# A layer with 32 sorted experts on one core: the choice of experts in two-operand steps, the rows sorted in two halves, five experts between

## What is computed

```python
def hierarchical_moe(h, w_router_group, b_router_group, w_router_expert, b_router_expert, w_gate, w_up, w_down):
    g_prob = softmax(t @ w_router_group + b_router_group)          # 4 groups
    g_p, g_idx = lax.top_k(g_prob, 1)
    e_logits = (t @ w_router_expert + b_router_expert).reshape(B * T, N_GROUPS, EXPERTS_PER_GROUP)
    e_in = jnp.einsum('ng,nge->ne', g_onehot, e_logits)            # the 8 experts of that group
    e_p, e_idx = lax.top_k(softmax(e_in), TOP_K_IN_GROUP)          # the best two, renormalised
    ...
    out = out + down(silu(t @ w_gate[e]) * (t @ w_up[e]) * combine[e])
```

## Time and profile before

| | |
|---|---|
| median of 3 runs | 869.36 us (866.34 to 869.45) |
| profiled execution | 869.71 us, span 867.8 us |
| PE, busy share of the span | 86% |
| DVE, ACT, POOL | 47%, 34%, 17% |
| DMA, mean over the span | 234 GB/s |
| DMA from about 650 us to 824 us | 416 to 420 GB/s |

### The profile page before, as it was taken

One profiled execution on the slowest core, in us unless ns is written; L12 is line 12 of the kernel. 1 busy time (PEld: TensorE's weight loads), 2 busy tenths in 40 slices (PEclk: granted clock), 3 DMA queues, 4 the chain that ended last, 5 costly groups with the idle time before them and its releaser, 6 DMA issues.

```text
span 867.8 us, 14573 instructions
## 1 busy us (share of the span) xinstructions
PE 750.1 (86%) x5476; PEld 598.7 (69%) x5476; DVE 403.9 (47%) x936; ACT 298.3 (34%) x550; POOL 143.9 (17%) x245
## 2 busy tenths in 40 slices
PE   2999999999888999998689999895789999778870
PEld 1899999997455698998577889894755555344430
DVE  3575324467444465665456567755652222111113
ACT  5433553556333264654322325444221111111110
POOL 5001000002233200232122100003012222211210
PEclk9999999999699999999999999997699999999995
DMA  5245243326587634535493637875399999999975
GB/s 185 98 147 182 97 147 122 122 97 204 150 243 209 198 135 146 191 117 190 151 299 127 220 107 261 352 297 216 147 374 416 419 418 418 419 420 419 419 284 188
DMA packets 38170, 202.84 MB, mean 234 GB/s; under 512 B 7490, under 2 KB 8018, under 8 KB 18898
## 3 DMA queue, kind: packets, MB, share of 16 engines
q1 hardware_dynamic: 24434, 160.29, 48.0%
q0 software_dynamic: 13664, 41.58, 15.0%
HBM read 184.24 MB, written 23.38 MB: 239 GB/s over the span
## 4 chain that ended last, share of the span: by engine, by line
PE 61%; DMA 16%; DVE 11%; ACT 5%; issue 5%; POOLq 0%; SPq 0%; POOL 0%; DVEq 0%; ACTq 0%
PE bank L1711 21%; PE bank L1715 10%; DMA fm<-in_w_moe 10%; PE bank L2059 7%; PE bank L1867 3%; PE bank L1701 3%; DMA em<-in_w_moe 3%; PE bank L2079 3%; DVE rm L1120 2%; ACT rm L797 2%; PE bank L1951 2%; PE bank L2040 2%; PE bank L1856 1%; DMA fm<-y_rows 1%; PE bank L1916 1%
## 5 line engine op out<-in xcount | busy, mean ns | idle before, releaser
L1711 PE MATMUL bank<-rm 128*128 128x320 f32 x1344 | 209.7, 315 | 1.6 <-ACT fm L825 1.6
L1711 PEld LDWEIGHTS bank<-rm 128*128 128x128 f32 x1344 | 201.3, 191 | 6.4 <-issue 3.7
L1120 DVE TENSOR_TENSOR rm<-fm,rm 128x2048 fp32r<-128x2048 f32 x48 | 110.0, 2292 | 71.1 <-ACT rm L797 70.6
L1715 PE MATMUL bank<-rm 128*128 128x256 f32 x960 | 122.2, 286 | 2.4 <-DVE fm L1491 2.4
L1715 PEld LDWEIGHTS bank<-rm 128*128 128x128 f32 x960 | 118.3, 193 | 3.3 <-issue 2.9
L2061 PE MATMUL bank<-fm,em 128*64 128x256 f32 x384 | 98.1, 401 | 0.0
L797 ACT ACTIVATE rm<-fm 128x2048 fp32r<-128x2048 f32 x48 | 91.9, 1915 | 17.1 <-PE bank L1711 11.2
L2059 PE MATMUL bank<-em 128*64 128x256 f32 x272 | 68.1, 395 | 12.9 <-DMA fm<-in_w_moe 7.9
L2059 PE MATMUL bank<-fm,em 128*64 128x256 f32 x240 | 60.3, 397 | 11.0 <-DMA fm<-in_w_moe 9.6
L2059 PEld LDWEIGHTS bank<-em 128*64 128x64 f32 x272 | 36.2, 140 | 40.2 <-issue 25.5
L1083 ACT ACTIVATE fm<-bank 64x256 f32<-64x256 f32 x32 | 12.0, 375 | 138.2 <-PE bank L2061 138.2
(11 more groups left out here) (391 smaller groups left out, 1010.5 us busy)
## 6 DMA issues: line engine op xcount, KB each, us to landing
fm<-in_w_moe SPq DMA_DIRECT2D x57, 1024.0 KB, 26.7
fm<-in_w_dense SPq DMA_DIRECT2D x48, 1024.0 KB, 4.9
em<-in_w_moe SPq DMA_DIRECT2D x39, 1024.0 KB, 25.7
fm<-in_state_C POOLq DMA_DIRECT2D x32, 257.0 KB, 4.4
out_C_sample<-fm POOLq DMA_DIRECT2D x32, 257.0 KB, 5.2
fm<-in_cache_v POOLq DMA_DIRECT2D x16, 512.0 KB, 4.6
fm<-in_cache_kT POOLq DMA_DIRECT2D x10, 512.0 KB, 5.8
em<-in_cache_kT POOLq DMA_DIRECT2D x6, 512.0 KB, 8.1
```

The costliest lines, as they stand in the source:

```text
L1120: s(TT(pair[c % 2][1], cube(raw[c % RAW1], KC), pair[c % 2][0], ALU.subtract), sem("split_done"))
L1711: ins = mm(bank[b][:, 0:NT], w[:, k, P * u:P * (u + 1)], a[:, k, :], start=first, stop=final)
L1715: ins = mm(bank[b][0:r, 0:CW], a[:, k, TILE0[u]:TILE0[u] + r], w[:, k, :], start=first, stop=final)
```

## The change

Four things are changed together.

1. **Choice of experts.** `gidx`, `eidx` and their casts are gone: the comparisons read the integer indices. The three `scalar_tensor_tensor` steps that push other groups down (one for each tile of tokens) become a product (`gneg` by a constant kept in `rb40`) and one sum over all three tiles.
2. **Low parts.** POOL makes the low part of `h2` for two tiles of tokens, DVE for the third (64 rows), after `gap`.
3. **Sort in two halves.** The one-hot rows are written by halves of 320 slots. PE sorts the first half (40 matmuls), expert 0 starts from it, and the second half is sorted in two pieces of 20 matmuls behind `down` of expert 1 and of expert 2, through banks 6 and 7. The offsets of experts 1 to 4 are limited so that their windows lie in the first half; from expert 5 on POOL waits for the whole of `xs`. DVE writes the second half's one-hot rows between its copies of the first half. The table of row numbers (L2098) goes behind `down` of expert 0, and the words for the end behind expert 1.
4. **Slots.** Loads 17 to 24 go into slots 0 to 7 again, each when its matrix is used up; 25 to 28 go to the memory of `h2s` and `onehot` when the second half is out (`xs_ready` at 2); later ones go round as before. Load 14 also waits for the first `onehot`. Small router tiles move from `fm` to that same memory.

```diff
@@ slots
+        NSLOT, NFREE, NAGAIN = len(slot), 17, 8
+        HALF, NBEFORE = SLOTS // 2, 5
+        h2s = [cube(rm[:, 0:3 * D], 3), cube(rm[:, 3 * D:5 * D], 2)]
+        def slot_of(n):
+            if n < NFREE:
+                return n
+            if n < NFREE + NAGAIN:
+                return n - NFREE
+            return n - NAGAIN if n < NSLOT + NAGAIN else slot_of(n - NSLOT)
@@ SP
-                    sp.wait_ge(sem("h2_split"), 3)
-                elif n == 17:
-                    sp.wait_ge(sem("sorted_full"), 2 * KC)
-                elif n >= NSLOT:
+                    sp.wait_ge(sem("h2_split"), 2)
+                    sp.wait_ge(sem("onehot"), 1)
+                elif n == NFREE + NAGAIN:
+                    sp.wait_ge(sem("xs_ready"), 2)
+                elif NFREE <= n < NFREE + NAGAIN:
+                    sp.wait_ge(sem("e_used"), n - NFREE + 1)
+                elif n >= NSLOT + NAGAIN:
@@ POOL
-            for t in range(3):
+            for t in range(2):
@@ ACT
+                if v in (2, 3):
+                    sorted_more((4 * (v - 2), 4 * (v - 2) + 2))
@@ DVE
-            s(CP(gidx, gi))
-            s(TT(ghot, iota[:, 0:NG].unsqueeze(1).broadcast_to([P, 3, NG]), gidx[:, :, 0:1].broadcast_to([P, 3, NG]),
+            s(TT(gneg, iota[:, 0:NG].unsqueeze(1).broadcast_to([P, 3, NG]), gi[:, :, 0:1].broadcast_to([P, 3, NG]),
                  ALU.not_equal))
+            s(TT(gneg, gneg, rb40[:, NG:NG + 1].unsqueeze(1).broadcast_to([P, 3, NG]), ALU.mult))
+            s(TT(esel.rearrange("p t (g e) -> p t g e", g=NG), gneg.unsqueeze(3).broadcast_to([P, 3, NG, EPG]),
+                 lg[:, :, 8:40].rearrange("p t (g e) -> p t g e", g=NG), ALU.add))
             for t in range(3):
-                s(STT(esel[:, t, :].rearrange("p (g e) -> p g e", g=NG),
-                      ghot[:, t, :].unsqueeze(2).broadcast_to([P, NG, EPG]), NEG,
-                      lg[:, t, 8:40].rearrange("p (g e) -> p g e", g=NG), ALU.mult, ALU.add))
                 s(v.max(etop[:, t, :], esel[:, t, :]))
                 s(v.max_index(ei[:, t, :], etop[:, t, :], esel[:, t, :]))
-            s(CP(eidx, ei))
...
+            dve.wait_ge(sem("h2_hi"), 3)
+            s(TT(h2s[0][NS:2 * NS, 2, :], h2[0:NS, 2, :], h2s[0][0:NS, 2, :], ALU.subtract))
...
+            for k in range(1, KC, 2):
+                dve.wait_ge(sem("sorted_full"), k + 1)
+                s(CP(xs[:, k, 0:HALF], bank[k % 4][:, 0:HALF]), sem("sorted_free_v"))
+                if k < 6:
+                    hot_slots(k // 2, 1)
+            dve.wait_ge(sem("sorted_free_a"), KC // 2)
+            s(v.tensor_reduce(most[:, 0:1], bank[4][:, 0:NE], AX_X, ALU.max), sem("xs_ready"))
...
+                if e in (2, 3):
+                    sorted_more((4 * (e - 2) + 1, 4 * (e - 2) + 3))
+                if e == 3:
+                    dve.wait_ge(sem("sorted_free_a"), KC)
+                    dve.wait_ge(sem("sorted_free_v"), KC)
+                    s(v.memset(xs[:, :, SLOTS:XC], 0.0), sem("xs_ready"))
@@ PE
             start(0)
-            pe.wait_ge(sem("onehot"), 3 + 6)
-            for k in range(2):
-                for t in range(3):
-                    i, r = 3 * k + t, ROWS[t]
-                    ins = mm(bank[6][0:CAP, 0:NE], at_rank[i][0:r, :], hot[k][0:r, t, :], start=(i == 0), stop=(i == 5))
-            ins.then_inc(sem("router_full"), 1)
...
                 down(4 + v % 2, htp[v % 2], weights(v, 2)).then_inc(sem("e_used"), 1)
+                if v == 0:
+                    row_table()
+                elif v in (1, 2):
+                    sort_more(range(4 * (v - 1), 4 * v))
```

More of the change, by code:

```diff
@@ L1065, in _, with sorted_more @@
             act.wait_ge(sem("x1_stored"), 16)
-            for n in range(0, 2 * KC, 2):
-                k, half = n // 2, n % 2
-                act.wait_ge(sem("sorted_full"), n + 1)
-                s(A_(xs[:, k, NT * half:NT * (half + 1)], bank[n % 4][:, 0:NT], ACT.Copy), sem("sorted_free_a"))
+            for k in range(0, KC, 2):
+                act.wait_ge(sem("sorted_full"), k + 1)
+                s(A_(xs[:, k, 0:HALF], bank[k % 4][:, 0:HALF], ACT.Copy), sem("sorted_free_a"))
+            def sorted_more(ks):
+                for k in ks:
+                    act.wait_ge(sem("sorted_full"), KC + k + 1)
+                    A_(xs[:, k, HALF:SLOTS], bank[6][:, 0:HALF], ACT.Copy).then_inc(sem("sorted_free_a"), 1)
             def take_y(v):
@@ L1566, in _, with hot_slots @@
             s(CP(place[NS:2 * NS, 2, :], place[0:NS, 2, :]))
+            def hot_slots(t, half):
+                w = slice(HALF * half, HALF * (half + 1))
+                s(TSC(onehot[:, t, w], iota[:, w], place[:, t, 0:1], None, ALU.is_equal))
+                s(STT(onehot[:, t, w], iota[:, w], place[:, t, 1:2], onehot[:, t, w], ALU.is_equal, ALU.add), sem("onehot"))
             for t in range(3):
-                s(TSC(onehot[:, t, :], iota, place[:, t, 0:1], None, ALU.is_equal))
-                s(STT(onehot[:, t, :], iota, place[:, t, 1:2], onehot[:, t, :], ALU.is_equal, ALU.add),
-                  sem("onehot"))
+                hot_slots(t, 0)
             dve.wait_ge(sem("router_full"), 5)
@@ L2034, in _, with sort, sort_more @@
                skip_group_check=True).then_inc(sem("router_full"), 1)
-            def sort(n, t):
-                k, half = n // 2, n % 2
+            def sort(b, k, half, t):
                 for i in range(2 if t < 2 else 1):
-                    ins = mm(bank[n % 4][:, 0:NT], h2s[i][:, t, P * k:P * (k + 1)],
-                             onehot[:, t, NT * half:NT * (half + 1)], start=(t == 0 and i == 0), stop=(t == 2))
+                    ins = mm(bank[b][:, 0:HALF], h2s[i][:, t, P * k:P * (k + 1)], onehot[:, t, HALF * half:HALF * (half + 1)],
+                             start=(t == 0 and i == 0), stop=(t == 2))
                 if t == 2:
                     ins.then_inc(sem("sorted_full"), 1)
+            pe.wait_ge(sem("h2_split"), 2)
             for t in range(3):
-                pe.wait_ge(sem("h2_split"), t + 1)
                 pe.wait_ge(sem("onehot"), t + 1)
-                for n in range(4):
-                    sort(n, t)
-            for n in range(4, 2 * KC):
-                pe.wait_ge(sem(("sorted_free_a", "sorted_free_v")[n % 2]), n // 2 - 1)
+                for k in range(4):
+                    sort(k, k, 0, t)
+            for k in range(4, KC):
+                pe.wait_ge(sem(("sorted_free_a", "sorted_free_v")[k % 2]), k // 2 - 1)
                 for t in range(3):
-                    sort(n, t)
+                    sort(k % 4, k, 0, t)
+            def sort_more(ks):
+                pe.wait_ge(sem("onehot"), 6)
+                for k in ks:
+                    if k >= 2:
+                        pe.wait_ge(sem(("sorted_free_a", "sorted_free_v")[k % 2]), KC // 2 + k // 2)
+                    for t in range(3):
+                        sort(6 + k % 2, k, 1, t)
             def gate_up(b, x, gate, up, between=None):
@@ L2091, in start, with row_table @@
                 last_u.then_inc(sem("e_used"), 1)
-            start(0)
-            pe.wait_ge(sem("onehot"), 3 + 6)
-            for k in range(2):
-                for t in range(3):
-                    i, r = 3 * k + t, ROWS[t]
-                    ins = mm(bank[6][0:CAP, 0:NE], at_rank[i][0:r, :], hot[k][0:r, t, :], start=(i == 0), stop=(i == 5))
-            ins.then_inc(sem("router_full"), 1)
+            def row_table():
+                pe.wait_ge(sem("onehot"), 6 + 6)
+                for k in range(2):
+                    for t in range(3):
+                        i, r = 3 * k + t, ROWS[t]
+                        ins = mm(bank[6][0:CAP, HALF:HALF + NE], at_rank[i][0:r, :], hot[k][0:r, t, :], start=(i == 0),
+                                 stop=(i == 5))
+                ins.then_inc(sem("router_full"), 1)
+            start(0)
             for v in range(NE):
```

87 lines of the change are left out of this document (42 added, 45 removed).

## The result

The changed kernel took 875.19 us in the median of five runs (871.57 to 876.79), the kernel before 869.36 (866.34 to 870.96). The ratio is 1.007, with a 95% interval of 1.0045 to 1.0095: 3.9 to 8.3 us slower. The forecast was 873.8 within 869.3 to 877.5.

What follows compares the result with a forecast made beforehand. The weight-load queue was taken to set the end, not PE: its last hole ends 4.4 us later, so the profiled 869.71 us becomes 874.1, and the median, 0.35 below, 873.8 us, within 869.3 to 877.5.

Steps and rivals of the forecast that it cites:

- (A): The forecast itself, the hole of the load queue at load 25: 2.5 to 6 us later, 55%.
- (C): Rival: PE's clock falls in a new pause, before expert 0 or 2: 875.5 for one, 877.2 for two, 17%.
- The choice: Choice of experts: new two-operand steps wait for POOL's low-part steps; chosen_r at 608.32 against 610.57, 2.25 us won.
- (B): Rival at the choice of experts: POOL spares the new steps, 3.16 us more won ahead of the sort, 870.6, 14%.
- The third low part: Low part moved to DVE, ahead of the sort: costs some 1.22 us, leaving 1.77 us of the 2.25 won.
- Expert 0: Start of the expert stage after the sort's first half: at 624.1 instead of 631.29, 7.2 us won.
- The queue: Weight loads: full flow at load 25 only at 656.2, 4.4 us later than before, after being idle twice.
- the table of rows ... expert 2 starts at 12.0 ... 30.45: Sum from expert 0's start to the second `xs_ready`: 30.45 us, with PE waiting 1.8 before expert 2.
- The instant to beat: When load 24 was in before the change, 71 loads being left: 651.8, with some 0.2 us for rows of `y_rows`.
- PE's own pace: PE in the expert stage: `down(3)` ends at 658.7 against 659.85, 1.1 us earlier, then starves later all the same.
- (D): Rival in the expert stage: PE, not the queue, sets the end, so the 1.1 us count, 868.3, 6%.
- (E): Rival: something faster that no row shows; over 0.5% needs load 25 flowing by 647.4, expert 0 at 615.3, 8%.

Runs made afterwards that it cites:

- three_operands: The changed kernel with the choice's product and sum as three scalar_tensor_tensor steps again, casts still gone: 875.29 us, ratio 1.0095.
- choice_only: The kernel before with the two-operand choice of experts alone, POOL keeping all three low parts, sort whole: 865.9 us, ratio 0.9965.
- sort_first: The kernel before with the new choice of experts and the third low part on DVE, sort whole: 865.77 us, ratio 0.9971.
- sort_first_pieces: The kernel before with the two-operand choice, third low part on DVE, POOL's low parts in eight pieces, sort whole: 866.09 us, ratio 0.9965.
- onehot_after: The changed kernel with the second half's one-hot rows written after the four copies of the first half, not between them: 874.32 us, ratio 1.0088.
- combined: The changed kernel with the second half one expert earlier, POOL's low parts in eight pieces and one-hot rows after the copies: 866.08 us, ratio 0.999.
- low_part_pieces: The changed kernel with POOL's two low-part steps of 128x1024 cut into eight of 128x256: 872.88 us, ratio 1.0076.
- early_filled: The changed kernel with second half one expert earlier, POOL's eight pieces, one-hot rows moved to DVE's waits, eight unread matmuls before expert 0: 864.85 us, 0.9947.

## Why the prediction was right, and where it was off

The direction, the range and the mechanism were right. The time alone doesn't tell (A) from (C), since 875.19 is inside the range of (A), 871.9 to 875.4, and 0.3 below what (C) gives for one fall; the traces do. The case that I called likeliest, (A) with the clock up, was not the regular one, and what I had as rival (C), at 17%, is.

**The choice.** Right in each step: 1.43 and 2.30 us for steps that need 0.2, the second spared in the gap, `chosen_r` within 0.13. `three_operands` shows that the form of the step doesn't matter. Rival (B) is out: in the rows shown, steps beside a step of POOL waited until it ended, and only those in the gap between two of its steps were spared. The Trainium skill's "SBUF — State Buffer", "Who interferes with whom", has the blocked step wait until the first is done; the traces agree, with the ends 0.05 us apart in `three_operands`. The integer operand, bounded by 0 and 0.6, costs 0.

**The third low part.** Right as a term: 1.22 us. It was taken in the sum as part of the change, without what it saves: the comparisons don't have to wait for a third step of POOL. By `choice_only` and `sort_first`, with POOL's steps counted from the same place, the two cancel (0.51 and 0.54 us, one profile of each), and the times don't differ either.

**Expert 0.** Right within 0.15, by the row of copies and one-hot pairs on DVE.

**The queue, where it was off.** The term that failed is "the table of rows ... expert 2 starts at 12.0 ... 30.45" after expert 0, in so far as it lets PE run at full clock. Measured is 32.89 to the issue, not 30.49. With the pauses filled it is 31.19, so 1.7 are the fall. Of the other 0.7, 0.6 are the two pieces of the sort, 3.25 and 3.24 us (in the chain) instead of 2.93. The two banks are not to blame as far as the trace goes: PE has no wait for a copy in either piece. The pace of a long row of matmuls is not that of a short one: the 13 unread matmuls, which wait for nobody, took 2.07 us, and 20 at that pace would take 3.2 (an estimate). The pause before expert 2, 1.62, was well sized (1.8).

Against that stands an error the other way. From the issue of load 17 to the last landing before were 205.08 us, from that of load 25 now 183.96: eight loads are worth 21.1 us, not 20.2. Part of it is in the sum itself: it put 0.2 us for rows of `y_rows`, but before, none of the 32 stores was out when load 17 went, and now three are out when load 25 goes (634.49, 643.29 and 652.27), which at the same 0.2 each is 0.6. The instant to beat was 0.9 later than I took. So 4.4, and 2.5 (2.4 behind expert 0 and 0.15 at its start), less 0.9, is 6.0, and 6.1 is seen.

**PE's own pace** was forecast to gain 1.1 us at `down(3)`. It ended at 659.67 in the changed kernel, 661.59 with the shift, which is 1.7 later than before: the fall and the longer pieces again. Nothing hangs on it, as the queue sets the end.

**The clock.** I gave (C) 17% with, for it, the fall at 836 to 838, and against it one pause of 1.38 us before expert 0. In the eight profiles of kernels with the sort in halves and pauses left open there was at least one fall each between expert 0 and load 25, two in three of them. Of six pauses of 2.2 to 2.4 us before expert 0 four were followed by one, and of six of 1.6 us before expert 2 five. All six of 1.37 to 1.38 us before expert 0 (before, `sort_first`, `sort_first_pieces`, `choice_only`, `onehot_after`, `combined`) were not, while both waits of 2.1 us in the last two of these were. The one row that I leaned on was a pause shorter than both of the new ones. The two pauses of over 2.2 us without a fall (after, `low_part_pieces`) came 5.1 us after the clock had risen in the sort (to the start of expert 0), the four with one 6.2 to 6.8 us after it; whether that matters no run tested.

Counted as forecast for one and two falls, (C) gave 875.5 and 877.2; the two profiles of the changed kernel have one and two, and the medians are 875.19 and 877.09. How many falls the executions without a profile had isn't on record, and the profile with one fall took 871.57, so that the medians fit this well is in part luck. What the traces carry is the 1.7 us for each fall.

**Rivals (D) and (E).** (D) is out: expert 0 starts 7 us earlier, PE is 1.7 us later at `down(3)` and not the 6.1 of the landing, and the time follows the last landing within 2 us in all thirteen rows of the table. PE's waits for weights are still there in the changed kernel from 600 to 850:

```profile
PE bank L2110 <- DMA em<-in_w_moe: 13.1, 7, 2.2
PE bank L2110 <- DMA fm<-in_w_moe: 11.7, 9, 2.3
```

(E) did not come about in the changed kernel. What it asked for, load 25 flowing by 647.4, `early_filled` reaches: 45.82 us after the router's end is 645.8 on the clock of before, and 1.62 later 647.4. It gets there by an earlier second half, not by an expert 0 at 615.3.

**Open.** Why one pause of 2.2 to 2.4 us is followed by a fall and another isn't; and whether `early_filled` is worth its trouble beside the whole sort with the new choice: its landing is 0.6 us earlier than that of `sort_first_pieces` (231.53 and 232.16), one profile of each.

## What to carry to other kernels

Find the last hole in a load queue that then runs without a break to the end: every microsecond ahead of it is one at the end (from issue to landing 204.7 to 205.1 us in the four kernels with the whole sort, 183.8 to 184.0 in the seven with the hole at load 25) until the hole is gone, and work that is started earlier elsewhere is worth nothing if what frees the memory for the loads comes later. When a long stage is cut so that a consumer can start early, look at what the whole stage used to release, and put its second part where that release is due, not where the consumer has a free place. And count each new pause of PE of some two microseconds at 1.7 more, until a profile shows that the clock stayed up.

## What was not expected of the hardware

- With matmuls that nobody reads in both pauses (13 of 128x320 in 2.07 us, and nine) the granted clock stayed at 1.00 in the one profile taken. Each fall that is missing there is worth 1.7 us.
- POOL's step of 128x1024 takes 2.4 us and one of 128x256 0.72 to 0.75, or 0.8 with the gap to the next (6.38 for eight): a quarter of the columns is a third of the time.
- From the issue behind a hole to the last of 71 loads were 183.80 to 183.96 us in seven profiles, with the clock of PE falling or not.
